# The end of a transformer block on one Trainium2 core: the norm's rows in groups of four blocks, each group in a PSUM bank of its own, and a square root of the first attention moved ahead of the last mask

## The chip, the core and the metric

The program runs on one core of one Trainium2 chip. Time is device microseconds (us) of one execution, from the first to the last instruction and what lies around them. The engines are TensorE (PE in the profile; PEld is its weight load), VectorE (DVE), ScalarE (ACT), GpSimd (POOL) and the DMA queue of SyncE (SP, SPq). Each runs its own list of instructions in order and waits on semaphores for the others.

## The reference, cut to what matters

Two transformer blocks follow one another, on 256 tokens of 1024 features in fp32. The change lies at the end of the first block's attention. The attention has two groups of heads, a retention and a difference of two softmaxes. Both are normed per head, joined, multiplied with `w_out`, gated and added to x; x is then normed and modulated, and a layer of product keys and experts begins with `hb @ w_query`.

```
x  = x + mod[:, 2] * (jnp.concatenate([ret_lat, diff_lat], axis=-1) @ w_out[layer])
h2 = modulate(x, norm2_g[layer], mod[:, 3], mod[:, 4])
x  = x + mod[:, 5] * peer_ffn(h2, peer_w_query[layer], ...)

def modulate(x, g, shift, scale):
    return rms_norm(x, g) * (1.0 + scale) + shift

out = merge_heads(rms_norm(y, g_norm) * (1.0 - lam_init))      # second group: diff_lat
scores = jnp.einsum('bhnid,bhnjd->bhnij', qc, kc) * intra_decay  # first group: a mask per head
```

## The kernel before, in words

Each fp32 product is made from two halves of each operand: ScalarE rounds a weight half of 128 x 1024 to `w_hi`, VectorE (for some halves GpSimd) subtracts to get `w_lo`, and TensorE runs three matmuls (hi by hi, hi by lo, lo by hi) into one PSUM region. The 257 weight chunks of 1 MB come in order through SyncE's queue into a ring of three (`raw`); chunk n waits until both halves of chunk n - 3 have been split. A half is numbered u: 40 to 47 are `w_out` (`U_OUT1`), 48 to 63 `w_query` (`U_QUERY`). On ScalarE and VectorE `ahead(u)` (L1401, L1853) makes every split up to half `REACH[u]`, about three beyond u; the ring of split halves has four places, so a split also waits for the matmuls of the half four before it.

The tokens are two tiles of 128 (i = 0, 1). The order of the attention is one list, `front_steps` (L149), which each engine walks for its own part of a step. `("win", p, h)` is a quarter of an input projection and brings `ahead` with it. `mask` n makes the decay mask of retention head n: VectorE two instructions, then ScalarE three exponentials; `madd` n is VectorE's sum of two of them. `rscore` n is TensorE's scores of head n, and VectorE's two products of scores and mask, which give the columns that `rweigh` n multiplies with v. `dvar`, `dnorm` are the norm of the second group: VectorE's scaling of sums, ScalarE's square root, VectorE's reciprocal and two products. `evac` 5 is ScalarE's silu of the last projection. `dblocks` transposes a gate and the four blocks of the second group (TensorE), which ScalarE and VectorE copy and split into `HC` (`high`, `low`); `out` n is the matmuls of half 40 + n of `w_out` with them. The last steps are `rweigh` 2 and 3, `rnorm`, `out` 2 and 3.

Then the four blocks of the first group are transposed (`block(TB_RET + k)`), each to a bank by `bank_of` (L788): banks 4, 5, 4, 5, so that the third waits until the first is split. `last_four` (L1049) runs the last four halves of `w_out`, first all for tile 0 (accumulators in banks 0, 1), then for tile 1 (banks 2, 3), with `turn_normed(0)` ahead of the last half of tile 1.

`normed` on ScalarE (L1461) and VectorE (L1928) is the end of the block. For a tile: VectorE adds the gated product to x (`add`, four instructions), ScalarE sums squares and takes the root (`squares`), VectorE inverts it and writes it on a diagonal (`inverse`), TensorE multiplies eight blocks of x by that diagonal (`turn_normed`, L1064), which transposes and scales them. Of each block an engine makes gain and shift (VectorE for even k, ScalarE for odd k) into `scaled4`, a ring of four, ScalarE rounds it into `HX`, and VectorE writes the rest. So a block passes three instructions and up to three waits. Tile 0 uses banks 0 and 1, tile 1 banks 2, 3, 0, 1 in turn (`norm_bank`, L774), with TensorE waiting for the blocks before. VectorE makes four blocks of tile 0, two of them ahead of `add(1)`, before it inverts the root of tile 1. The first half of `w_query` (`feat_half(48)`, L1130) needs, block by block, both tiles' rows in `HX`.

SyncE's queue has, between chunk 27 and chunk 28, the copy `x_keep <- x`, which waits for x of tile 1 (L820).

Of the kernel before, what the change touches and what calls it, by code (L numbers as in the profile page):

```python
# [7 lines left out]
F32 = mybir.dt.float32  # L8
# [140 lines left out]
def front_steps():  # L149
# [63 lines left out]
    win(5, 3, ("added", 1), ("rscore", 1), ("mask", 3), ("madd", 2), ("dnorm", 0), ("evac", 5))  # L213
# [156 lines left out]
def turned_at(i, k):  # L370

    return 8 * i + k + 1


def bank_turned(i, k):

    return turned_at(i, k if i else 7)


def both_turned(j, k):  # L380

    return 16 + 8 * (j - 1) + k + 1
# [5 lines left out]
def program(nc, wall, keys_d, cols_d, rows_d, bigrows_d, crow_d, wmod_d, dist_d, x_d, ctx_d, pT_d, gws_d, out_d, n_chunks):  # L388
    assert n_chunks * 2 == U_END
    with ExitStack() as es:  # L390
# [240 lines left out]
        scaled4 = fsc[:, 0:2, :].rearrange("p a (b t) -> p (a b) t", b=2)  # L631
# [142 lines left out]
        def norm_bank(i, k):  # L774

            if i == 0:
                return PB[k % 2][:, (k // 2) * 128:(k // 2 + 1) * 128]
            return PB[[2, 3, 0, 1][k % 4]][:, 0:128]
# [5 lines left out]
        def norm_half(s_, i, k):  # L784
            return HX[:, s_, k, i * 128:(i + 1) * 128]


        def bank_of(n):  # L788
            for first, banks in ((TB_Y, (4, 5, 6, 7)), (TB_U, (6, 7)), (TB_RET, (4, 5)),
                                 (TB_DIFF, (0, 1, 2, 3))):  # L790
                if n >= first:
                    return banks[(n - first) % len(banks)], n - len(banks) if n - first >= len(banks) else None
# [71 lines left out]
        def tensor_program(e):  # L864
# [199 lines left out]
            def turn_normed(i):  # L1064
# [3 lines left out]
                for k in range(8):  # L1068
                    if i and k >= 4:
                        t.wait_ge(s_nl, turned_at(1, k - 4))  # L1070
                    elif i and k >= 2:
                        t.wait_ge(s_nl, turned_at(0, 7))
                    t.did(mm(norm_bank(i, k), x[:, i, k * 128:(k + 1) * 128], dgn[:, i, :], True, True), s_nt)
# [56 lines left out]
            def feat_half(u, out, j=None):  # L1130
# [3 lines left out]
                for k in range(8):  # L1134
                    if j is not None:
                        t.wait_ge(s_nl, both_turned(j, k) if j else turned_at(1, k))
# [252 lines left out]
        def scalar_program(e):  # L1389
# [58 lines left out]
            def normed_highs(i, ks):  # L1448

                for k in ks:  # L1450
                    if k % 2:
                        a.wait_ge(s_nt, bank_turned(i, k))
                        if 8 * i + k >= 4:
                            a.wait_ge(s_nl, 8 * i + k - 3)
                        act(scaled4[:, k % 4, :], norm_bank(i, k), ACT.Identity, scale=G2[:, k:k + 1],
                            bias=modT[:, 24 + k, 0:1])
                    else:
                        a.wait_ge(s_nf, 4 * i + k // 2 + 1)
                    act(norm_half(0, i, k), scaled4[:, k % 4, :], ACT.Copy, sig=s_nh)

            def normed(last, scr_):  # L1461

                squares(N_PEER, 0, scr_)
                ahead(last - 2)
                ahead(last - 1)
                normed_highs(0, range(2))
                squares(N_PEER, 1, scr_)
                normed_highs(0, range(2, 8))
                ahead(last)
                normed_highs(1, range(8))  # L1470
# [349 lines left out]
        def vector_program(e):  # L1820
# [92 lines left out]
            def normed_lows(i, ks):  # L1913


                def difference(k):
                    v.wait_ge(s_nh, turned_at(i, k))
                    tt(norm_half(1, i, k), scaled4[:, k % 4, :], norm_half(0, i, k).bitcast(F32), SUB, sig=s_nl, free=True)

                for k in ks:  # L1920
                    if k % 2 == 0:
                        v.wait_ge(s_nt, bank_turned(i, k))
                        ts(scaled4[:, k % 4, :], norm_bank(i, k), G2[:, k:k + 1], modT[:, 24 + k, 0:1], MUL, ADD, sig=s_nf)
                    if k > ks[0]:
                        difference(k - 1)
# [791 lines left out]
```

## Time and profile before

| | us |
|---|---|
| median of three runs | 1788.83 |
| fastest and slowest of the three | 1788.52, 1795.13 |
| the profiled execution | 1793.46 |
| its span | 1791.7 |

| engine | busy us | share |
|---|---|---|
| TensorE | 1666.4 | 93% |
| VectorE | 1254.2 | 70% |
| ScalarE | 909.8 | 51% |
| GpSimd | 84.2 | 5% |

The profiled execution took 4.6 us more than the median, 1.8 of it outside its span. TensorE's busy time is that of an engine whose instructions overlap, so it is no measure of full speed; where it stands still, and at which clock it runs, says more. The mean granted clock is 0.97 of full speed.

### The profile page before, as it was taken

The page shows a single profiled execution, that of the slowest core. Times are in us where ns is not written, and L with a number is a line of the kernel's source. Part 1 is how long each engine was busy: PE and PEld are TensorE (multiplying, and loading weights), DVE is VectorE, ACT ScalarE, POOL GpSimd, SP SyncE. Part 2 cuts the span into 40 slices and gives each one's busy share as a digit, 9 for nine tenths or more (in the row PEclk, how much of TensorE's full clock was granted, in tenths as well). Part 3 has the DMA queues.
Part 4 walks back from the last instruction along what each step waited for, and adds up shares of the span by engine and source line. Part 5 has one row for each costly group of instructions (what it writes and reads, how often), then busy time and mean ns, then how long its engine had stood idle before and what let it go on. Part 6 is the DMA issues. An engine that isn't in the chain of part 4 may idle for free.

```text
span 1791.7 us, 29060 instructions
## 1 busy us (share of the span) xinstructions
PE 1666.4 (93%) x11518; PEld 1492.9 (83%) x11518; DVE 1254.2 (70%) x2040; ACT 909.8 (51%) x1206; POOL 84.2 (5%) x50
## 2 busy tenths in 40 slices
PE   6898787999999899988999999999998888999996
PEld 6676566998999788867999999899998777899995
DVE  5886655899888899976666555665556885655555
ACT  3454445554555455534444444544446766544445
POOL 1100002622000000000000000000000000000000
PEclk9898888999999999999999999999999998999998
DMA  6743333446655355637555555454543532555541
GB/s 262 275 168 133 106 110 123 144 165 200 205 182 199 141 201 202 220 133 267 211 199 211 198 189 186 154 200 177 191 185 130 212 130 106 190 193 188 188 171 64
DMA packets 53418, 318.52 MB, mean 178 GB/s; under 512 B 5953, under 2 KB 6113, under 8 KB 19362
## 3 DMA queue, kind: packets, MB, share of 16 engines
q1 hardware_dynamic: 52098, 310.60, 48.7%
q0 software_dynamic: 1184, 6.05, 0.9%
q8 instruction: 91, 1.49, 0.3%
q14 instruction: 45, 0.37, 0.1%
HBM read 307.17 MB, written 9.47 MB: 177 GB/s over the span
## 4 chain that ended last, share of the span: by engine, by line
PE 61%; DVE 25%; ACT 10%; issue 2%; DMA 2%; DVEq 0%; SPq 0%; ACTq 0%
PE pb L868 60%; DVE w_lo L1827 7%; DVE ar L1827 7%; ACT w_hi L1399 4%; ACT ar L1399 3%; DVE ar L1839 2%; DMA raw<-in_wall 1%; DVE HC L1827 1%; DVE ar L2181 1%; ACT L1399 1%; ACT HC L1399 1%; DVE ar L2178 1%; DVE ar L1984 1%; DVE raw L1984 1%; DVE ar L1981 1%
## 5 line engine op out<-in xcount | busy, mean ns | idle before, releaser
L1827 DVE TENSOR_TENSOR w_lo<-raw,w_hi 128x1024 fp32r<-128x1024 f32 x467 | 572.3, 1225 | 277.3 <-ACT w_hi L1399 251.8
L868 PE MATMUL pb<-HX,w_hi 128*128 128x256 f32 x3904 | 716.7, 285 | 12.2 <-DVE w_lo L1827 10.7
L1399 ACT ACTIVATE w_hi<-raw 128x1024 fp32r<-128x1024 f32 x498 | 528.2, 1061 | 346.2 <-PE pb L868 297.9
L868 PEld LDWEIGHTS pb<-HX,w_hi 128*128 128x128 f32 x3904 | 614.0, 193 | 19.7 <-DVE w_lo L1827 10.3
L868 PE MATMUL pb<-HX,w_lo 128*128 128x256 f32 x1952 | 553.9, 284 | 0.0
L868 PE MATMUL pb<-w_hi,HC 128*128 128x512 f32 (+1 forms) x1648 | 530.8, 393 | 11.7 <-DVE HC L1827 11.2
L868 PEld LDWEIGHTS pb<-HX,w_lo 128*128 128x128 f32 x1952 | 375.9, 193 | 0.0
L868 PEld LDWEIGHTS pb<-w_hi,HC 128*128 128x128 f32 x1648 | 312.0, 190 | 76.4 <-DVE w_lo L1827 12.5
L868 PE MATMUL pb<-w_lo,HC 128*128 128x512 f32 (+1 forms) x824 | 322.4, 391 | 0.0
L1827 DVE TENSOR_TENSOR ar<-ar 128x512 bf16<-128x512 bf16 (+8 forms) x470 | 247.5, 563 | 59.3 <-ACT ar L1399 30.9
L1399 ACT ACTIVATE ar<-pb 128x512 f32<-128x512 f32 (+3 forms) x203 | 112.7, 555 | 242.6 <-PE pb L868 154.9
L868 PE MATMUL pb<-w_hi,HX 128*128 128x512 f32 x512 | 177.7, 416 | 13.2 <-DVE w_lo L1827 5.6
L868 PEld LDWEIGHTS pb<-w_lo,HC 128*128 128x128 f32 x824 | 156.6, 190 | 29.4
L868 PE MATMUL pb<-ar 128*128 128x64 bf16 (+3 forms) x1960 | 134.1, 228 | 26.4 <-DVE ar L1827 8.7
L868 PEld LDWEIGHTS pb<-ar 128*128 128x128 bf16 (+2 forms) x1960 | 111.7, 124 | 50.7 <-issue 26.8
L868 PEld LDWEIGHTS pb<-w_hi,HX 128*128 128x128 f32 x512 | 102.4, 200 | 38.2 <-issue 11.4
L1399 ACT ACTIVATE HC<-ar 128x512 fp32r<-128x512 f32 x87 | 55.0, 632 | 103.8 <-PE pb L868 60.7
L868 PE MATMUL pb<-w_lo,HX 128*128 128x512 f32 x256 | 104.4, 408 | 0.0
L1827 DVE TENSOR_TENSOR HC<-ar,HC 128x512 fp32r<-128x512 f32 x87 | 60.3, 693 | 46.6 <-ACT HC L1399 42.8
L2565 POOL TENSOR_TENSOR w_lo<-raw,w_hi 128x1024 fp32r<-128x1024 f32 x31 | 75.7, 2442 | 158.5 <-ACT w_hi L1399 117.9
L1399 ACT ACTIVATE ar<-ar 128x512 f32<-128x512 f32 (+7 forms) x85 | 50.3, 591 | 57.5 <-DVE ar L1839 23.8
L868 PEld LDWEIGHTS pb<-w_lo,HX 128*128 128x128 f32 x256 | 51.3, 201 | 9.7
(139 smaller groups left out, 716.1 us busy)
## 6 DMA issues: line engine op xcount, KB each, us to landing
raw<-in_wall SPq DMA_DIRECT2D x257, 1024.0 KB, 4.8
ar<-in_wmod SPq DMA_DIRECT2D x24, 512.0 KB, 3.7
act_keep<-ar SPq DMA_DIRECT2D x28, 256.0 KB, 5.6
ar<-act_keep SPq DMA_DIRECT2D x28, 256.0 KB, 5.1
x<-in_wmod SPq DMA_DIRECT2D x8, 512.0 KB, 3.3
ar<-in_bigrows POOLq DMA_DIRECT2D x2, 1024.0 KB, 5.1
ar<-acs_keep POOLq DMA_DIRECT2D x2, 1024.0 KB, 8.4
ar<-in_crow SPq DMA_DIRECT2D x2, 512.0 KB, 5.9
```

The lines of the kernel that those rows point to most:

```text
L868: return e.matmul(o, l, r, start=start, stop=stop, skip_group_check=True)
L1399: a.did(e.activation(out, in_, func, scale=scale, **kw), sig)
L1827: v.did(e.tensor_tensor(out, a_, b_, op), sig)
L1839: v.did(e.scalar_tensor_tensor(out, a_, s_, b_, op0, op1), sig)
L1981: v.did(e.scalar_tensor_tensor(junk, w, 1.0, crow_ctx, MUL, MUL, accum_out=modT[:, n, 1:2]))
L1984: v.did(e.scalar_tensor_tensor(w, w, 1.0, c_, MUL, MUL, accum_out=modT[:, n, 0:1]), s_modv)
L2178: v.did(e.max(vals[:, c_], src))
L2181: v.did(e.max_index(idx[:, c_], vals[:, c_], src))
L2565: p.did(e.tensor_tensor(w_lo[:, made % NH, :], raw_half(w), w_hi[:, made % NH, :].bitcast(F32), SUB), s_lop)
```

## The change

Five edits. In the list of steps, `dnorm` and `evac` 5 go ahead of `mask` 3 and `madd` 2, `dnorm` also ahead of `rscore` 1. The four blocks of the first group get banks 4, 5, 7, 6. VectorE's splits of the half that `ahead(43)` makes (half 46) move behind the second of those blocks' splits. The norm's rows of a tile get two banks, even k in one and odd k in the other, for each tile its own; a wait is for four blocks, `scaled8` keeps all sixteen (in space that `qT` takes later), and the rounding and its rest are one instruction for four blocks. On VectorE `add(1)` comes ahead of all `low`s of tile 0, and the splits of halves 49 and 50 come last; on ScalarE the split of half 49 comes after `squares` of tile 1. The first `feat_half` takes k in the order 0, 2, 4, 6, 1, 3, 5, 7.

```diff
-    win(5, 3, ("added", 1), ("rscore", 1), ("mask", 3), ("madd", 2), ("dnorm", 0), ("evac", 5))
+    win(5, 3, ("added", 1), ("dnorm", 0), ("rscore", 1), ("evac", 5), ("mask", 3), ("madd", 2))
...
-        scaled4 = fsc[:, 0:2, :].rearrange("p a (b t) -> p (a b) t", b=2)
+        scaled8 = qTf[:, 0:2048].rearrange("p (i k t) -> p i k t", i=2, k=8)
...
         def norm_bank(i, k):
-            if i == 0:
-                return PB[k % 2][:, (k // 2) * 128:(k // 2 + 1) * 128]
-            return PB[[2, 3, 0, 1][k % 4]][:, 0:128]
+            return PB[2 * i + k % 2][:, (k // 2) * 128:(k // 2 + 1) * 128]
...
-            for first, banks in ((TB_Y, (4, 5, 6, 7)), (TB_U, (6, 7)), (TB_RET, (4, 5)),
+            for first, banks in ((TB_Y, (4, 5, 6, 7)), (TB_U, (6, 7)), (TB_RET, (4, 5, 7, 6)),
...
                 t.wait_ge(s_nd, 4 + i + 1)
-                for k in range(8):
-                    if i and k >= 4:
-                        t.wait_ge(s_nl, turned_at(1, k - 4))
-                    elif i and k >= 2:
-                        t.wait_ge(s_nl, turned_at(0, 7))
-                    t.did(mm(norm_bank(i, k), x[:, i, k * 128:(k + 1) * 128], dgn[:, i, :], True, True), s_nt)
+                for odd in range(2):
+                    for k in range(odd, 8, 2):
+                        ins = mm(norm_bank(i, k), x[:, i, k * 128:(k + 1) * 128], dgn[:, i, :], True, True)
+                    t.did(ins, s_nt)
...
-                for k in range(8):
+                for k in (0, 2, 4, 6, 1, 3, 5, 7) if j == N_PEER else range(8):
                     if j is not None:
-                        t.wait_ge(s_nl, both_turned(j, k) if j else turned_at(1, k))
+                        t.wait_ge(s_nl, both_turned(j, k) if j else group_turned(1, k % 2))
...
+            def normed_scaled(i):
+
+                a.wait_ge(s_nt, group_turned(i, 1))
+                for k in range(1, 8, 2):
+                    act(scaled8[:, i, k, :], norm_bank(i, k), ACT.Identity, scale=G2[:, k:k + 1], bias=modT[:, 24 + k, 0:1],
+                        free=k > 1)
+
+            def normed_highs(i):
+
+                a.wait_ge(s_nf, i + 1)
+                for odd in range(2):
+                    act(norm_group(0, i, odd), scaled8[:, i, odd::2, :], ACT.Copy, sig=s_nh)
 
             def normed(last, scr_):
 
                 squares(N_PEER, 0, scr_)
                 ahead(last - 2)
+                normed_scaled(0)
+                normed_highs(0)
+                squares(N_PEER, 1, scr_)
                 ahead(last - 1)
-                normed_highs(0, range(2))
-                squares(N_PEER, 1, scr_)
-                normed_highs(0, range(2, 8))
+                normed_scaled(1)
+                normed_highs(1)
                 ahead(last)
-                normed_highs(1, range(8))
...
+            def normed_scaled(i):
+
+                v.wait_ge(s_nt, group_turned(i, 0))
+                for k in range(0, 8, 2):
+                    ts(scaled8[:, i, k, :], norm_bank(i, k), G2[:, k:k + 1], modT[:, 24 + k, 0:1], MUL, ADD,
+                       sig=s_nf if k == 6 else None)
+
+            def normed_lows(i):
+
+                for odd in range(2):
+                    v.wait_ge(s_nh, group_turned(i, odd))
+                    tt(norm_group(1, i, odd), scaled8[:, i, odd::2, :], norm_group(0, i, odd).bitcast(F32), SUB, sig=s_nl,
+                       free=True)
...
                 ahead(last - 2)
-                ahead(last - 1)
-                normed_lows(0, range(2))
+                normed_scaled(0)
                 v.wait_ge(s_used, used(last))
                 add(1)
-                normed_lows(0, range(2, 4))
+                normed_lows(0)
                 inverse(N_PEER, 1)
-                normed_lows(0, range(4, 8))
-                normed_lows(1, range(8))
+                normed_scaled(1)
+                normed_lows(1)
+                ahead(last)
...
-                elif name == "out":
+                elif name == "out" and n < 3:
                     ahead(U_OUT1 + n)
...
-            turn(TB_RET, 4)
+            for k in range(4):
+                low(TB_RET + k)
+                if k == 1:
+                    ahead(U_OUT1 + 3)
             ahead(U_OUT1 + 4)
```

## Rows read from the trace of the kernel before

**Rows 1.** The chain that ended last, in order of time: start, us, what

```profile
240.55 12.54 PE pb L868 x64
...
291.02 54.14 PE pb L868 x442
```

**Rows 2.** TensorE in order of time: start, us, operation, count, [idle before, its releaser]

```profile
221.83 6.94 PE L868 MATMUL pb<-ar 64*128 64x256 f32 x24 [1.64 <-DVE ar L1839]
229.75 3.97 PE L868 MATMUL pb<-ar 64*128 64x256 f32 x24 [0.98 <-DVE ar L1839]
238.05 0.38 PE L946 MATMUL pb<-cols,modT 128*8 128x128 f32 x1 [4.33 <-ACT ar L1399]
```

**Rows 3.** TensorE, the same view: `rscore` 3, `out` 1, `rweigh` 2

```profile
244.58 1.99 PE L868 MATMUL pb<-ar 64*128 64x256 f32 x8
246.50 0.51 PE L868 MATMUL pb<-w_hi,HC 128*128 128x512 f32 x1
...
249.34 3.73 PE L868 MATMUL pb<-ar 128*128 128x128 f32 x32
```

**Rows 4.** ScalarE in order of time, around the last mask and the square root

```profile
225.96 1.06 ACT L1399 ACTIVATE w_hi<-raw 128x1024 fp32r<-128x1024 f32 x1
231.91 0.63 ACT L1399 ACTIVATE ar<-ar 128x512 f32<-128x512 f32 x1 [4.89 <-DVE ar L1839]
...
233.84 1.28 ACT L1399 ACT_TABLE_LOAD   x1
...
236.71 1.29 ACT L1399 ACTIVATE ar<-pb 128x512 f32<-128x512 f32 x2
```

**Rows 5.** VectorE in order of time, the same stretch

```profile
229.00 1.49 DVE L1839 SCALAR_TENSOR_TENSOR ar<-pb,ar 128x512 f32<-128x512 f32 x2
...
235.61 1.42 DVE L1827 TENSOR_TENSOR ar<-ar,sm 128x512 f32<-128x512 f32 x2
```

**Rows 6.** Windows of 2 us; the third number from the right is the granted clock

```profile
222.00:224.00 2.00, 2.00 (x7) 1.58 (x8) 1.81 (x3) 0.01 (x1) 0.00 (x0) 0.61 0.90 274
...
242.00:244.00 2.00, 2.00 (x8) 1.61 (x7) 1.23 (x1) 0.16 (x1) 0.00 (x0) 0.77 0.63 219
...
260.00:262.00 2.00, 0.43 (x3) 0.28 (x4) 1.81 (x3) 0.00 (x0) 0.00 (x0) 1.00 0.56 147
...
280.00:282.00 2.00, 0.00 (x0) 0.00 (x0) 1.05 (x2) 1.48 (x5) 0.00 (x0) 0.61 0.31 131
...
294.00:296.00 2.00, 2.00 (x18) 2.00 (x18) 1.86 (x2) 0.60 (x2) 0.00 (x0) 0.97 0.03 8
```

**Rows 7.** VectorE in order of time, at the first group's blocks

```profile
259.80 1.23 DVE L1827 TENSOR_TENSOR w_lo<-raw,w_hi 128x1024 fp32r<-128x1024 f32 x1
260.94 0.87 DVE L1839 SCALAR_TENSOR_TENSOR HC<-pb,cols,HC 128x256 fp32r<-128x256 f32 x2
```

**Rows 8.** TensorE in order of time, from there to the first half of `w_query`

```profile
261.56 0.80 PE L881 MATMUL pb<-cols,ar 128*128 128x128 f32 x4 [2.56 <-DVE HC L1839]
...
272.50 2.02 PE L868 MATMUL pb<-fsc,x 128*128 128x128 f32 x16 [0.58 <-DVE fsc L1832]
...
284.02 1.19 PE L868 MATMUL pb<-fsc,x 128*128 128x128 f32 x4 [8.08 <-DVE fsc L1832]
...
291.47 0.77 PE L868 MATMUL pb<-HX,w_hi 128*128 128x256 f32 x2
```

**Rows 9.** VectorE and ScalarE in order of time, in the norm

```profile
277.78 0.69 DVE L1827 TENSOR_TENSOR ar<-pb,ar 128x512 f32<-128x512 f32 x1
...
276.55 0.46 ACT L1399 ACTIVATE fsc<-pb,modT,sm 128x128 f32<-128x128 f32 x1
...
281.43 0.29 ACT L1399 ACTIVATE sm<-sm 128x1 f32<-128x1 f32 x1
```

**Rows 10.** SyncE's queue, and a DMA group (KB each, us to landing)

```profile
280.67 0.33 SPq L822 DMA_DIRECT2D x_keep<-x  x1
...
ar<-in_ctx SPq DMA_DIRECT2D x1, 1024.0 KB, 14.2
```

More of the change, by code:

```diff
@@ L367, in result, with group_turned @@
     return 4 * j + 2 * i + half + 1
[L370 to L377, printed above, removed]
+def group_turned(i, odd):
+    return 2 * i + odd + 1
 def both_turned(j, k):
-    return 16 + 8 * (j - 1) + k + 1
+    return 4 + 8 * (j - 1) + k + 1
 CTX_AT = {0: -256, 1: 256 - 512, 4: 768 - 2048, 5: 1280 - 2560}
@@ L774, in norm_bank, with norm_group @@
         def norm_bank(i, k):
-            if i == 0:
-                return PB[k % 2][:, (k // 2) * 128:(k // 2 + 1) * 128]
-            return PB[[2, 3, 0, 1][k % 4]][:, 0:128]
+            return PB[2 * i + k % 2][:, (k // 2) * 128:(k // 2 + 1) * 128]
         def rows_bank(k):
             return PB[k // 4 * 2 + k % 2][:, k // 2 % 2 * 256:k // 2 % 2 * 256 + 256]
-        def norm_half(s_, i, k):
-            return HX[:, s_, k, i * 128:(i + 1) * 128]
+        def norm_group(s_, i, odd):
+            return HX[:, s_, odd::2, i * 128:(i + 1) * 128]
         def bank_of(n):
-            for first, banks in ((TB_Y, (4, 5, 6, 7)), (TB_U, (6, 7)), (TB_RET, (4, 5)),
+            for first, banks in ((TB_Y, (4, 5, 6, 7)), (TB_U, (6, 7)), (TB_RET, (4, 5, 7, 6)),
                                  (TB_DIFF, (0, 1, 2, 3))):
@@ L1446, in squares @@
                 act(root_[:, i:i + 1], rs[:, 2 * i + 1:2 * i + 2], ACT.Sqrt, bias=part[:, i:i + 1], sig=s_std)
[L1448 to L1459, printed above, removed]
+            def normed_scaled(i):
[7 more added lines that the diff above has]
+                    act(norm_group(0, i, odd), scaled8[:, i, odd::2, :], ACT.Copy, sig=s_nh)
             def normed(last, scr_):
@@ L1911, in inverse @@
                 ts(dgn[:, i, :], ident, root_[:, i:i + 1], sig=s_nd)
[L1913 to L1925, printed above, removed]
-                difference(ks[-1])
+            def normed_scaled(i):
[8 more added lines that the diff above has]
+                       free=True)
             def normed(last, add):
```

## The prediction

> **What bounds the kernel now.** I read the chain of waits in order of time first, then the time orders of TensorE, ScalarE and VectorE from 216 to 312 us, then the windows. The chain lies on TensorE through `out` 0 to `rweigh` 3, and again for 54 us from 291.02 [rows 1]; between these it runs over ScalarE and VectorE, and there TensorE stands still. That is where the change works. TensorE waits 4.33 us until 238.05 for the silu of `evac` 5 [rows 2, 4], 2.56 us until 261.56 for the bank of the first group's first block, and 8.08 us until 284.02 for the diagonal of tile 1 [rows 8]. After 291 nothing in the stretch takes up a shift: VectorE's and GpSimd's work there hangs on TensorE's scores, so what is won ahead of 291 I carry to the end whole.
>
> Of the clock the rows show this. The windows have a mean of 0.61 in 222 to 224, where it falls to 1.2 GHz after TensorE was idle for 1.64 us and began on score products; 0.77 in 242 to 244, where it comes back, over 4 us after TensorE took up work at 238.05; 1.00 in 260 to 262 in spite of 2.56 us of idleness; 0.61 in 280 to 282, in the long stop; 0.97 in 294 to 296 [rows 2, 6, 8]. The same 24 records of `rscore` and `rweigh` take 3.97 us at full clock and 6.94 nearly all at the low one [rows 2].
>
> **Part A, `dnorm` and `evac` 5 ahead of mask 3.** ScalarE is free at 225.96 + 1.06 = 227.02 and then waits 4.89 us for mask 3 [rows 4]. Now a table load of 1.28 and a square root go there (done about 228.6), then the load for silu and the silu of 1.29 (done about 231.2); the exponentials of mask 3 may need a third load. TensorE's `evac` wait is thus gone. Against it, VectorE makes `dnorm`'s reciprocal and products (1.42 and some 0.3 around them) before `rscore` 1's products, which move from 229.00 to 230.75, and all behind them by 1.75: mask 3 begins on ScalarE at 233.65 instead of 231.91 [rows 4, 5]. A third load would run from 231.3 to 232.6, before the mask is there: nothing, with 1.0 us of cover left. The exponentials end at 235.5, `madd` 3 at 236.7.
>
> TensorE's `rscore` 2 moves from 229.75 to 231.5, after a gap of 2.7 instead of 0.98 us, and ends with `rweigh` 1 at 235.5 if the clock holds, at up to 238.4 if it falls (3.97 or 6.94 from there [rows 2]). `dblocks` began at 238.05. So `out` 0, which began at 240.55 [rows 1], begins 2.95 us earlier if the clock holds (`madd` 3 and two splits then end last, at 237.7), 0.1 to 0.3 earlier if it falls, and 0.9 us later at worst, if the first half of `rscore` 2 is slow too. The fall at 222 came after a shorter gap, before the same kind of products, so I take the fall. But TensorE is then busy from 231.5 on without the long stop, and the clock is back for `out` 0: that took 240.55 to 244.58 = 4.03 us, while `out` 1 took 246.50 to 249.34 = 2.84 [rows 1, 3]: 1.2 us won. **A = 0.15 + 1.2 = 1.35 us, bounds -0.9 and +4.1.** What is late next is TensorE itself.
>
> The Trainium skill, ScalarE: Activation LUTs, "What ACT_TABLE_LOAD costs", speaks against this reordering: it puts each switch of tables at 2.66 us, a drain on top of the load. Here two loads, a root and the gaps fit between 233.84 and 236.71, 2.87 us [rows 4], so no such drain is seen. By the page the exponentials would end about 3 us later, and A would be near 0; the row decides.
>
> **Part B, banks 4, 5, 7, 6.** The third and fourth block are transposed right behind the first two, which costs TensorE 0.7 us inside its wait. The split of half 46 took 1.23 us ahead of the first block's two splits, which ran 260.94 to 261.81 [rows 7]. Now they begin at 259.8 and TensorE's first half of `last_four` needs the first alone, while before it stood behind the fourth block, which waited for the second: it began about 262.1, and now 259.8 + 0.44 + 0.1 = 260.35, 1.75 us earlier. The moved split ends near 262.0, its half is wanted at 263.1; the split of half 47 (ScalarE at 261.0, VectorE at 262.95) ends at 264.2, its half is wanted at 264.4. That cover is thin: 0.2 us. **B = 1.75, bounds 1.4 and 1.9.**
>
> **Part C, the norm.** All times here are those of the trace, before the shifts. The diagonal of tile 0 is there at 272.4, TensorE's eight blocks end at 274.4 [rows 8]. VectorE splits half 48 alone until 274.3 (one of two splits leaves the path, 1.24 us), makes four scalings (0.45 apart, which is ScalarE's 0.46 for the same block [rows 9]: 276.1), and starts `add(1)` at 276.15 instead of 277.78 [rows 9]; TensorE's last half of `w_out` for tile 1 ends before that, 1.4 us (half of `out` 1) behind 274.4. ScalarE in that time makes four gains (0.46 each, overlapping by 0.09: 1.6) and two roundings of 128 x 512 (0.63 each by the nearest row of that size [rows 4]), and is free at 277.5, before the first half of x at 277.6. The root of tile 1, ended at 281.72 [rows 9], ends at 280.1. Then VectorE writes the diagonal at once (its two group splits lie before, under the root), at 280.95 instead of 283.87, where two more blocks stood ahead of it. TensorE starts tile 1 at 281.1 instead of 284.02 [rows 8].
>
> From there: before, 7.45 us to the first `w_query` matmul at 291.47. Now eight blocks at the low clock (2.02 at full clock, so 3.75 and some latency, until 284.9; the row of 1.19 for two of them agrees [rows 8]), four gains on ScalarE 1.6, rounding of the even group 0.65, its split 0.75 [rows 5], and 0.15 of latency: 288.1. The grouping itself wins next to nothing (0.4 us), because TensorE must finish all eight before ScalarE begins; the win is the diagonal's. So 3.3 us. The clock: before, TensorE was half busy from 284 and full speed came at about 294.1, 2.7 us into `w_query` [rows 6, 8]; now there is a gap of 3.2 us right before, so I allow up to 4 us of low clock, which costs 0 to 0.7 us more. **C = 3.0, bounds 1.8 (the whole first half at the low clock) and 3.9 (full clock within 1.5 us).** What is late next is again ScalarE's and VectorE's pass over tile 1. Of the splits that moved, half 49's ends at 290.0, wanted at about 292.5; half 50's at 291.3, wanted after 295. Behind them in SyncE's queue hangs chunk 27, which now starts when half 49 is split, at 290, and not at about 275.6 (two splits of 1.23 behind the rounding of half 48), with `x_keep` (280.67 [rows 10]) and chunk 28 behind it. Its first half, 54, is rounded once half 50 is used up: 288.1 and three halves of 2.9 us (54.14 us hold sixteen of them and their key scores [rows 1]) and 1 for the clock, about 298. That is a cover of 8 us. I cost it at nothing.
>
> **Sum.** 1.35 + 1.75 + 3.0 = 6.1 us. Against the profiled execution, 1793.46, that is 1787.4; the median of the runs lies 4.6 us lower, and against it 1788.83 - 6.1 = **1782.7 us**, 0.34% less. A measurement of this kernel tells about 0.5% (8.9 us) from no change.
>
> **The rivals.**
> 1. *The front gives back what it won.* VectorE's 1.75 us ahead of `rscore` 1 and a clock that stays low through `rweigh` 1 and `dblocks`: A = -0.9, the rest as above. 3.9 us, 1784.9. For it: 1.64 us were enough for the fall at 222 [rows 2, 6]. Against: TensorE has 6 to 7 us of work on end before `out` 0.
> 2. *The clock holds* in the 2.7 us gap, as in the 2.56 at 260 [rows 6, 8]: A = 4.1, C towards 3.5, 9.4 us, 1779.4, past the bound. Against: the work after that earlier gap was of full height, here it is products of 64 rows.
> 3. *Slower: chunk 27 lands late.* It has 8 us. The longest landing of a transfer of 1 MB was 14.2 us, with a full queue [rows 10]. Each us past 8 stops ScalarE's rounding and TensorE behind it; from 14.1 us on the sum of 6.1 is gone, and 23 us make the kernel over 0.5% slower, 1797.8. Here only `x_keep` and chunk 28 share the queue, and they come behind it.
> 4. *No shift reaches the end*: the VectorE chain from 345 us on or the ring of chunks takes it up: 1788.8. Against it: VectorE is idle up to TensorE's scores in all of the stretch before, as the chain's 54 us on TensorE say [rows 1].
>
> **How the numbers follow.** Forecast 0.58; rival 1 0.20; rival 2 0.11; rival 3 0.03; rival 4 0.08. The extremes of the bounds are 2.3 and 9.9 us, that is 1786.5 and 1778.9; three runs of one kernel were 6.6 us apart, upwards of the fastest, so the range is 1777 to 1789. Faster by over 0.5% is rival 2 and the edge of the forecast, where B and C come at their upper bounds: 0.18. Slower by over 0.5% is rival 3 and the spread: 0.03. Within 0.5%: 0.79.
>
> **What would show it.** Right: VectorE's products of `rscore` 1 come 1.75 us later than before, no 4.33 us stop of TensorE ahead of `dblocks`, full clock in `out` 0; no stop of 2.56 us at the first group's blocks; 15.6 us from TensorE's blocks of tile 0 (272.50) to the first `w_query` matmul (291.47), instead of 19.0 [rows 8]. Wrong: ScalarE waiting for chunk 27, a stop of TensorE for half 47 or 49, or a stretch from 291 to 345 that is longer than 54 us.

## The result, and the profile after

| | before | after |
|---|---|---|
| median of 20 runs each, us | 1794.97 | 1788.52 |
| lowest and highest | 1788.19, 1798.89 | 1784.83, 1794.38 |
| the profiled execution | 1793.46 | 1791.86 |
| its span | 1791.7 | 1790.1 |
| its mean granted clock | 0.970 | 0.967 |

The ratio is 0.9972, with a 95% interval of 0.9961 to 0.9982: the change wins 5.0 us (3.2 to 7.0), more than nothing and less than 0.5%. The two medians lie 6.4 us apart, inside that interval. I had said 6.1 us, and 1782.7 as the time. The size of the gain lies in the interval; the time is 5.8 us too low, because the median of three that I subtracted from, 1788.83, was a low draw of a kernel whose median over 20 runs is 1794.97. From that level 1782.7 would be a gain of 12.3 us, over twice the 5.0 measured. Of the 20 runs of before only three are under 1790, and two of the three that I had are among them.

The two profiled executions differ by 1.6 us only, which is less than the change wins in the stretch it touches. So first where the win stands, by points that both traces have. "Split" is the start of VectorE's split of half 41 at 219 us, the last work that the change leaves alone.

| us | before | after | won | said |
|---|---|---|---|---|
| A: split to `rscore` 3 | 24.84 | 24.19 | 0.65 | 1.35 |
| B: to the first addition to x | 23.30 | 21.44 | 1.86 | 1.75 |
| C: to the first `w_query` matmul | 23.59 | 20.05 | 3.54 | 3.3 |
| C, to the end of two `w_query` halves | 30.78 | 27.56 | 3.22 | 3.0 |
| from there to a memset of the expert layer | 439.10 | 438.09 | 1.01 | 0 |
| split to that memset | 518.02 | 511.28 | 6.74 | 6.1 |
| the mixer, first to last table load (about 1340 to 1567 us) | 221.93 | 226.82 | -4.89 | 0 |

A, B and C, to the end of two halves, win 5.73 us. The last 1.01 us up to the memset lies in work that the change leaves alone: in before the granted clock is 0.77 in 445 to 450 us and 0.89 in 450 to 455, in after it is 1.00 in both; in the eleven other kernels below the same piece takes 437.2 to 438.0 us.

TensorE in order of time, after, in the columns of [rows 2]:

```profile
221.00 3.97 PE L863 MATMUL pb<-ar 64*128 64x256 f32 x24 [1.65 <-DVE ar L1833]
230.68 7.33 PE L863 MATMUL pb<-ar 64*128 64x256 f32 x24 [5.71 <-DVE ar L1833]
237.84 0.27 PE L941 MATMUL pb<-cols,modT 128*8 128x128 f32 x1
...
240.17 0.47 PE L863 MATMUL pb<-w_hi,HC 128*128 128x512 f32 x1 [1.19 <-DVE HC L1833]
...
256.99 1.03 PE L876 MATMUL pb<-cols,ar 128*128 128x128 f32 x8
...
277.71 3.75 PE L863 MATMUL pb<-fsc,x 128*128 128x128 f32 x16 [5.13 <-DVE fsc L1826]
284.60 0.48 PE L863 MATMUL pb<-HX,w_hi 128*128 128x256 f32 x2 [3.14 <-DVE HX L1821]
```

The stop of 4.33 us ahead of `dblocks` is gone [rows 2], but the one ahead of `rscore` 2 has grown to 5.71 us. The stop of 2.56 us at the first group's blocks is gone, with the four blocks (eight records) in one piece at 256.99; 0.79 us is left behind them. The stop ahead of tile 1's blocks went from 8.08 to 5.13 us, and a new one of 3.14 stands in front of `w_query` [rows 8].

ScalarE in order of time, after, where the square root now stands:

```profile
226.26 1.28 ACT L1392 ACT_TABLE_LOAD   x1
227.56 0.21 ACT L1392 ACTIVATE sm<-sm 128x8 f32<-128x8 f32 x1
227.84 1.28 ACT L1392 ACT_TABLE_LOAD   x1
229.13 1.29 ACT L1392 ACTIVATE ar<-pb 128x512 f32<-128x512 f32 x2
230.50 1.28 ACT L1392 ACT_TABLE_LOAD   x1
232.83 0.63 ACT L1392 ACTIVATE ar<-ar 128x512 f32<-128x512 f32 x1 [1.05 <-DVE ar L1833]
```

The third load ends 1.05 us before mask 3 is there.

Windows of the clock, after, in the columns of [rows 6]:

```profile
226.00:228.00 2.00, 0.00 (x0) 0.00 (x0) 1.68 (x4) 1.84 (x4) 0.00 (x0) 0.87 0.00 0
228.00:230.00 2.00, 0.00 (x0) 0.00 (x0) 1.73 (x5) 1.90 (x3) 0.00 (x0) 0.50 0.00 0
```

In the 5.71 us stop the granted clock falls to 1.2 GHz, and the 24 records after it take 7.33 us.

TensorE's piece of the chain at `w_query` and behind it is 54.01 us, where it was 54.14 [rows 1]. At the memset after is 7.56 us ahead of before (730.20 against 737.76), of which 0.82 lay ahead of the split; at the first table load of the mixer it is 6.64 us ahead (1339.29 against 1345.93). In the mixer of the second block, which the change leaves alone, this one execution loses 4.89 us again. The same 24 matmuls behind the same stop, before and then after:

```profile
1451.43 2.89 PE L868 MATMUL pb<-ar 128*128 128x64 f32 x24 [1.96 <-DVE ar L1827]
```

```profile
1445.96 5.36 PE L863 MATMUL pb<-ar 128*128 128x64 f32 x24 [1.96 <-DVE ar L1821]
```

The windows of 5 us there, before and then after:

```profile
1445.00:1450.00 5.00, 4.47 (x20) 3.38 (x18) 4.55 (x6) 4.75 (x6) 0.00 (x0) 1.00 0.64 210
1450.00:1455.00 5.00, 3.56 (x28) 3.43 (x29) 4.82 (x4) 3.80 (x4) 0.00 (x0) 1.00 0.00 0
```

```profile
1445.00:1450.00 5.00, 4.04 (x19) 4.04 (x20) 4.79 (x5) 3.33 (x4) 0.00 (x0) 0.60 0.01 2
1450.00:1455.00 5.00, 5.00 (x16) 4.20 (x16) 4.65 (x5) 0.00 (x0) 0.00 (x0) 0.50 0.68 223
```

Once the clock stayed at 2.4 GHz, once it fell. From the table load ahead of this stop to the next it is 13.45 us in before (1447.93 to 1461.38) and 18.28 in after (1442.46 to 1460.74), so 4.83 of the 4.89 us are lost here. It is one of several places at which the mixer's time scatters, as the experiments show.

### The profile page after: what moved, and what is told of

Same layout as the page of the kernel before. It is cut to its first block, busy times and chain, and to the rows that moved or that the text cites. A ratio compares the mean times of both kernels' runs of the same rounds, so it can differ in the third digit from the quotient of the medians.

```text
span 1790.1 us, 29024 instructions
## 1 busy us (share of the span) xinstructions
PE 1668.2 (93%) x11518; PEld 1495.9 (84%) x11518; DVE 1252.1 (70%) x2028; ACT 908.1 (51%) x1195; POOL 83.5 (5%) x50
## 3 DMA queue, kind: packets, MB, share of 16 engines
q0 software_dynamic: 1184, 6.05, 0.8%
## 4 chain that ended last, share of the span: by engine, by line
PE 65%; DVE 20%; ACT 10%; DMA 2%; issue 2%; SPq 0%; DVEq 0%; ACTq 0%
PE pb L863 64%; DVE w_lo L1821 5%; DVE ar L1821 5%; ACT w_hi L1392 4%; ACT ar L1392 3%; DVE ar L1833 2%; DMA ar<-act_keep 1%; DVE ar L2177 1%; ACT L1392 1%; DMA raw<-in_wall 1%; ACT HC L1392 1%; DVE HC L1821 1%; DVE ar L1977 1%; DVE ar L2174 1%; DVE raw L1977 1%
## 5 line engine op out<-in xcount | busy, mean ns | idle before, releaser
L863 PE MATMUL pb<-w_hi,HC 128*128 128x512 f32 (+1 forms) x1648 | 530.0, 393 | 14.6 <-DVE HC L1821 12.3
```

The costliest lines, as they stand in the source:

```text
L863: return e.matmul(o, l, r, start=start, stop=stop, skip_group_check=True)
```

## The experiments

The theory: the three parts are independent stretches whose wins add, 0.65, 1.9 and 3.5 us; part A is small because VectorE's 1.75 us of `dnorm` stand ahead of `rscore` 1 and TensorE then runs `rscore` 2 and `rweigh` 1 at the low clock; part C is won by the order on VectorE, not by the groups. Its rivals: the parts overlap or depend on one another; A's loss has another cause; C is won by the groups. Each experiment is read by the stretches of the table above in its own trace, which are sharper than the times, and then by its time.

**The front alone.** The kernel before, with one line of the change.

```diff
-    win(5, 3, ("added", 1), ("rscore", 1), ("mask", 3), ("madd", 2), ("dnorm", 0), ("evac", 5))
+    win(5, 3, ("added", 1), ("dnorm", 0), ("rscore", 1), ("evac", 5), ("mask", 3), ("madd", 2))
```

> The kernel before with the list of steps reordered alone (root and evac 5 ahead of mask 3, root ahead of rscore 1). Measured on the stretch from VectorE's split that precedes the first head's score products to the start of rscore 3 on TensorE: 24.84 us in the trace before, 24.19 after the whole change. Theory 1 (TensorE's stop ahead of dblocks goes, but VectorE's 1.75 us ahead of rscore 1's products hold TensorE back at the low clock): 23.4 to 24.5, and the later stretches as before the change (23.3 us from rscore 3 to the first addition to x, 23.6 from there to the first w_query matmul). Theory 2 (the reordering is free, the clock came by chance): 20.7 to 22. Theory 3 (it costs): 25.5 or more. Time: 0 to 2 us less than before.

Measured: 1794.64 us, ratio 1.0008 (0.9997 to 1.0019). A took 24.21 us, as in after. But B took 24.98 and not 23.30: against the trace of before A won 0.63 us and B lost 1.68. TensorE in order of time and the windows, of this kernel:

```profile
260.16 0.80 PE L881 MATMUL pb<-cols,ar 128*128 128x128 f32 x4 [2.55 <-DVE HC L1839]
```

```profile
260.00:262.00 2.00, 1.84 (x9) 1.47 (x10) 1.20 (x4) 1.21 (x3) 0.00 (x0) 0.92 0.93 377
262.00:264.00 2.00, 2.00 (x6) 1.52 (x6) 1.33 (x2) 0.80 (x1) 0.00 (x0) 0.50 0.26 107
```

The stop of 2.55 us is the one of before [rows 8], but here the clock fell behind it, to 0.50 in 262 to 264, and `last_four` began slowly. In the trace of before it had stayed at full, 1.00 in 260 to 262 [rows 6]. Moving the front alone shows no gain in time.

**The banks alone.** The kernel before, with the banks and the later split of half 46.

```diff
-            for first, banks in ((TB_Y, (4, 5, 6, 7)), (TB_U, (6, 7)), (TB_RET, (4, 5)),
+            for first, banks in ((TB_Y, (4, 5, 6, 7)), (TB_U, (6, 7)), (TB_RET, (4, 5, 7, 6)),
...
-                elif name == "out":
+                elif name == "out" and n < 3:
...
-            turn(TB_RET, 4)
+            for k in range(4):
+                low(TB_RET + k)
+                if k == 1:
+                    ahead(U_OUT1 + 3)
```

> The kernel before with the four banks of the first group's blocks and the moved split of half 46 alone. From the start of rscore 3 to VectorE's first addition to x: 23.30 us before, 21.44 with the whole change. If the stop was the bank's and the split's alone: 21.4 to 21.6 here, and nothing in the other stretches. If part of it came from the shift of the other edits (clock, queue): 22 to 23.3. Time: 1.8 us less.

Measured: 1791.57 us, ratio 0.9991 (0.9981 to 1.0000). B took 21.44 us as in after, A and C (24.61, 23.60) about what they took before (24.84, 23.59). But its front, which has the old order, does not look like [rows 2]:

```profile
229.59 7.49 PE L868 MATMUL pb<-ar 64*128 64x256 f32 x24 [3.95 <-DVE ar L1839]
237.89 0.38 PE L946 MATMUL pb<-cols,modT 128*8 128x128 f32 x1 [0.81 <-ACT ar L1399]
```

Here `rscore` 1 and `rweigh` 0 took 3.97 us and not 6.94, so the stop ahead of `rscore` 2 is 3.95 us and not 0.98; the clock fell in it, `rscore` 2 and `rweigh` 1 took 7.49, and only 0.81 us of the 4.33 us stop ahead of `dblocks` is left. The next kernel has the same rows. In all twelve traces other than that of before the 24 records of `rscore` 1 and `rweigh` 0 took 3.97 us.

**The norm alone.** The kernel after, with the first two parts undone.

```diff
-    win(5, 3, ("added", 1), ("dnorm", 0), ("rscore", 1), ("evac", 5), ("mask", 3), ("madd", 2))
+    win(5, 3, ("added", 1), ("rscore", 1), ("mask", 3), ("madd", 2), ("dnorm", 0), ("evac", 5))
...
-            for first, banks in ((TB_Y, (4, 5, 6, 7)), (TB_U, (6, 7)), (TB_RET, (4, 5, 7, 6)),
+            for first, banks in ((TB_Y, (4, 5, 6, 7)), (TB_U, (6, 7)), (TB_RET, (4, 5)),
...
-            for k in range(4):
-                low(TB_RET + k)
-                if k == 1:
-                    ahead(U_OUT1 + 3)
+            turn(TB_RET, 4)
```

> The kernel before with the new norm alone (groups of four in banks of their own, second tile added first, moved splits). From the first addition to x to the first w_query matmul: 23.59 us before, 20.05 with the whole change. If the norm's edit stands by itself: 19.9 to 20.2 here. The first two halves of w_query may hold up to 1 us more of the low clock than before. Time: 2 to 3.5 us less.

Measured: 1791.66 us, ratio 0.9977 (0.9968 to 0.9987). C took 20.03 us, as in after; A 24.60; B 24.96, for here too the clock fell behind the old stop. A window of this kernel:

```profile
262.00:264.00 2.00, 2.00 (x7) 1.56 (x7) 1.25 (x3) 1.50 (x2) 0.00 (x0) 0.62 0.63 266
```

So the parts do not depend on one another: each shortens its own stretch alone as it does with the others, A by 0.63, B by 1.86 and C by 3.56 us, in sum 6.05, against 0.65, 1.86 and 3.54 with all of them. By time the three ratios sum to -0.24%, the whole is -0.28%, each known to about 0.1% only. The stretches next to the edited one do move, though by the clock: B rose by 1.7 us in two of the three. From the split to the memset the three kernels are shorter by 0.2, 3.3 and 2.9 us, in sum 6.4, and by 6.7 with all parts; that this fits so well is luck, because 1.0 to 1.9 us of each of these numbers is the piece behind `w_query`, which was slow in the trace of before. And B is worth more than its trace of before says: with the old banks it took 23.30 or 24.96 to 24.98, with the new ones 21.43 to 21.47 in the ten traces with them.

**Groups without the order.** The kernel after, with the split of half 49 and the differences of tile 0 ahead of `add(1)` again; on ScalarE, not shown, the split of half 49 goes ahead of tile 0's rows again.

```diff
                 ahead(last - 2)
+                ahead(last - 1)
                 normed_scaled(0)
+                normed_lows(0)
                 v.wait_ge(s_used, used(last))
                 add(1)
-                normed_lows(0)
```

> The changed kernel with the grouping kept and the order undone: both splits ahead of tile 0's scaling, tile 0's group splits ahead of the addition for tile 1. Theory 1 (the order wins, the grouping nothing): the addition for tile 1 starts 2.5 to 3.5 us later than in the changed kernel, and the stretch from the first addition to x to the first w_query matmul is 23.0 to 24.0 us, that of the kernel before. Theory 2 (the grouping wins by fewer waits): 21.5 or less. Time: 2.5 to 4 us more than the changed kernel.

Measured: 1792.01 us, ratio 0.9984 (0.9975 to 0.9994). C took 23.22 us: of the 3.54 us only 0.37 are left. From the diagonal of tile 1 to the first `w_query` matmul it is 7.32 us, as in after, against 7.89 before. In its parts, the 3.54 us of C are 1.55 from `add(0)` to `add(1)` (9.90 to 8.35), 1.42 from `add(1)` to the diagonal (5.80 to 4.38) and 0.57 behind the diagonal. In this kernel they are 11.72, 4.18 and 7.32 us. So the 0.57 us stay with the groups, and without the order the first two parts together win nothing. This is not the order of before: all of tile 0 is ahead of `add(1)` here and nothing of it behind, so `add(1)` comes 1.82 us later than there, and the diagonal follows sooner. TensorE in order of time, of this kernel:

```profile
279.47 3.75 PE L863 MATMUL pb<-fsc,x 128*128 128x128 f32 x16 [8.30 <-DVE fsc L1826]
286.36 0.77 PE L863 MATMUL pb<-HX,w_hi 128*128 128x256 f32 x2 [3.14 <-DVE HX L1821]
```

The long stop ahead of tile 1's blocks is back, 8.30 us, as before's 8.08 [rows 8].

**The root ahead of mask 3, but behind `rscore` 1.** The kernel after, with one step moved.

```diff
-    win(5, 3, ("added", 1), ("dnorm", 0), ("rscore", 1), ("evac", 5), ("mask", 3), ("madd", 2))
+    win(5, 3, ("added", 1), ("rscore", 1), ("dnorm", 0), ("evac", 5), ("mask", 3), ("madd", 2))
```

> The changed kernel with dnorm behind rscore 1 instead of ahead of it (order: added, rscore 1, dnorm, evac 5, mask 3, madd 2). If VectorE's 1.75 us ahead of rscore 1's products are what hold TensorE back: those products start 1.7 us earlier, rscore 2 and rweigh 1 with them, and the stretch from the split ahead of the first score products to the start of rscore 3 is 22.4 to 23.0 us instead of 24.19. If mask 3 and madd 3, which stay where they are, bind instead: 23.8 to 24.3. Time: 0 to 1.7 us less than the changed kernel.

Measured: 1787.58 us, ratio 0.9955 (0.9939 to 0.9971). A took 22.72 us, 1.47 less than after. TensorE in order of time, of this kernel:

```profile
221.48 3.97 PE L863 MATMUL pb<-ar 64*128 64x256 f32 x24 [1.62 <-DVE ar L1833]
229.40 7.49 PE L863 MATMUL pb<-ar 64*128 64x256 f32 x24 [3.95 <-DVE ar L1833]
...
239.23 0.47 PE L863 MATMUL pb<-w_hi,HC 128*128 128x512 f32 x1 [0.41 <-DVE HC L1833]
```

The stop is 3.95 instead of 5.71 us, 1.76 less, which is `dnorm`'s time on VectorE. The clock falls all the same and the 24 records still take 7.49 us. ScalarE's order and its three table loads are those of after. The two kernels with the old front have the same stop and the same 7.49 us, and A took 24.61 and 24.60 there: `dnorm` and `evac` 5 ahead of mask 3 win 1.9 us, and `dnorm` ahead of `rscore` 1 gives 1.5 to 1.7 of it back (A is 24.19 to 24.43 in the five traces that have it there without idle matmuls in front).

**Tile 1 block by block, the order kept.** The kernel after, with single waits for tile 1 and banks 2, 3, 6, 7 in turn; tile 0 keeps its groups. The diff is TensorE's part; ScalarE and VectorE do gain, rounding and rest of tile 1 for each block.

```diff
         def norm_bank(i, k):
+            if i:
+                return PB[[2, 3, 6, 7][k % 4]][:, 0:128]
             return PB[2 * i + k % 2][:, (k // 2) * 128:(k // 2 + 1) * 128]
...
+                if i:
+                    for k in range(8):
+                        if k >= 4:
+                            t.wait_ge(s_nl, block_turned(k - 4))
+                        t.did(mm(norm_bank(1, k), x[:, 1, k * 128:(k + 1) * 128], dgn[:, 1, :], True, True), s_nt)
+                    return
...
-                for k in (0, 2, 4, 6, 1, 3, 5, 7) if j == N_PEER else range(8):
+                for k in range(8):
```

> The changed kernel with tile 1's norm block by block again (four banks in turn, a wait for each block, gain, rounding and split block by block), tile 0 in groups, the order of the change kept. Theory 1 (grouping makes TensorE, ScalarE and VectorE take turns, so it costs on tile 1): the first w_query matmul comes about 4 us behind the diagonal of tile 1 instead of 7.0, and the first half of w_query ends 2.5 to 4 us earlier, since the last block is then waited for. Theory 2 (waits per block cost what turns cost): 6.5 to 7.5 us, no difference. Time by theory 1: 2 to 4 us less than the changed kernel.

Measured: 1784.62 us, ratio 0.9945 (0.9929 to 0.9961). The diagonal of tile 1 to `w_query` takes 5.00 us instead of 7.32, and C 17.72: theory 1, with 2.3 us won to the end of two halves (27.56 to 25.28). TensorE in order of time, of this kernel:

```profile
276.31 4.92 PE L873 MATMUL pb<-fsc,x 128*128 128x128 f32 x16 [5.12 <-DVE fsc L1852]
280.88 0.77 PE L873 MATMUL pb<-HX,w_hi 128*128 128x256 f32 x2
```

The blocks take longer on TensorE, 4.92 instead of 3.75 us, since they wait for banks; but the first matmul of `w_query` follows without a stop, because the first blocks have been rounded and split by then. The groups' 3.14 us stop is the price of having all eight blocks and their gains before the first rounding, on the path that ends last. Single waits alone are not what helps: the kernel before had them too and took 7.89 us, because VectorE still had four blocks of tile 0 behind the diagonal, and TensorE stood 2.02 us at 287.23 for a bank that tile 0 held. Four banks and the new order came together with the single waits here; which of them is worth how much was not taken apart.

**TensorE kept at work.** The kernel after, with idle matmuls of an identity into an unused bank: 4 and 10 of them ahead of `rscore` 1 and 2, 10 ahead of tile 1's blocks and 5 behind.

```diff
+            def warm(bank, n):
+                for _ in range(n):
+                    mm(PB[bank][:, 0:128], ident, ident, True, True)
...
+                    if n in (1, 2):
+                        t.wait_ge(s_wev, group_done(1))
+                        warm(2, 4 if n == 1 else 10)
...
+            warm(5, 10)
...
+            warm(5, 5)
```

> The changed kernel with additional 128 x 128 matmuls of the identity into an unused bank, whose result nobody reads: 4 ahead of rscore 1, 10 ahead of rscore 2, 10 ahead of tile 1's blocks, 5 behind them. Each costs about 0.24 us at full clock, all inside TensorE's stops. If the low clock after the stops is what the remaining time hangs on: granted clock 1.00 throughout, rscore 2 and rweigh 1 in about 4 us instead of 7.3, tile 1's eight blocks in 2.0 instead of 3.75, the first half of w_query in 2.9 instead of 4.4; together 4 to 6 us less than the changed kernel. If the clock falls nevertheless, the additional matmuls run at half speed and cost 1 to 4 us.

Measured: 1785.12 us, ratio 0.9951 (0.9937 to 0.9964). TensorE in order of time, of this kernel:

```profile
225.16 2.40 PE L863 MATMUL pb<-cols 128*128 128x128 f32 x20
231.04 6.60 PE L863 MATMUL pb<-ar 64*128 64x256 f32 x24 [3.47 <-DVE ar L1842]
...
277.52 2.02 PE L863 MATMUL pb<-fsc,x 128*128 128x128 f32 x16 [2.87 <-DVE fsc L1835]
```

Ten (20 records, 2.40 us) were too few in front: 3.47 us of stop are left, and the products still take 6.60, so A is 23.64, only 0.55 less than after. In the norm ten were enough: tile 1's blocks take 2.02 us and not 3.75, and C is 18.30 instead of 20.05. The 4 to 6 us expected did not come: it is 3.4 by the medians, and 2.4 from the split to the memset (511.28 to 508.86).

**Both better orders.** Block by block for tile 1 (its diff is the one above), and with it:

```diff
-    win(5, 3, ("added", 1), ("dnorm", 0), ("rscore", 1), ("evac", 5), ("mask", 3), ("madd", 2))
+    win(5, 3, ("added", 1), ("rscore", 1), ("dnorm", 0), ("evac", 5), ("mask", 3), ("madd", 2))
```

> The changed kernel with both earlier edits together: dnorm behind rscore 1, and tile 1's norm block by block. They lie in different stretches, so they should add: 22.7 us from the split ahead of the first score products to rscore 3, about 5 us from the diagonal of tile 1 to the first w_query matmul. Stretch from that split to GpSimd's memset in the expert layer: 506 to 507.5 us (511.3 in the changed kernel, 518.0 before). Time: 4 us less than the changed kernel, ratio to before 0.993 to 0.996.

Measured: 1784.02 us, ratio 0.9933 (0.9910 to 0.9955). A is 22.76, B 21.46, C 17.72, each as in the kernel that had it alone. The two add up by the stretches; by the times they come out within the scatter of the single ones.

**All three.** The last one, with idle matmuls.

```diff
+                    if n in (1, 2):
+                        t.wait_ge(s_wev, group_done(1))
+                        warm(2, 4 if n == 1 else 12)
...
+            warm(5, 16)
```

> The kernel of e8 with additional 128 x 128 matmuls of the identity into unused banks, which nobody reads: 4 ahead of rscore 1, 12 ahead of rscore 2, 16 ahead of tile 1's blocks. If the low clock is what is left: full clock through rscore 2 and rweigh 1 (4 us for the 24 records instead of 7.5), and through tile 1's blocks and the first half of w_query. Stretch from the split to the memset: 502 to 505 us, time 2 to 4 us less than e8. If the clock falls all the same, as it did in the front of the previous such kernel, 0 to 1.5 us.

Measured: 1781.52 us, ratio 0.9934 (0.9910 to 0.9958). TensorE in order of time, of this kernel:

```profile
224.72 2.84 PE L873 MATMUL pb<-cols 128*128 128x128 f32 x24
228.83 5.19 PE L873 MATMUL pb<-ar 64*128 64x256 f32 x24 [1.27 <-DVE ar L1868]
```

With the stop down to 1.27 us the 24 records take 5.19 instead of 7.49, not the 4 expected, and A falls to 20.90: 3.3 us less than after. C is 17.41, hardly less than 17.72, for block by block TensorE waits for the other engines anyway, and the clock is 0.50 again from 276 us on. Split to memset: 504.68 against 507.24.

**The mixer's stop.** The kernel after, with idle matmuls ahead of two groups of heads, which cover the stop at 1446.

```diff
+                    if n <= 4:
+                        t.wait_ge(s_xs, 8)
+                        warm(6, 3 if n == 0 else 7)
```

> The changed kernel with additional matmuls of the identity in the second block's mixer, far behind the change: 3 ahead of the first heads' products, 7 ahead of the next four's, in TensorE's stops of 0.6 and 2.0 us there. The stretch between the first and last table load of that part has the same work in every kernel so far and took 219.1 to 226.8 us (221.9 in the trace before, 226.8 in the changed one, where the clock fell at 1447 for 10 us). If the clock after that stop is what took the profiled gain back: 219 to 224 us here, no fall within 15 us of the heads' products, and 0 to 3 us less than the changed kernel in the mean. If something else took it: 224 to 228 us.

Measured: 1789.14 us, ratio 0.9973 (0.9958 to 0.9988), that of the change itself. The stop was closed and the clock held there, by TensorE in order of time:

```profile
1447.09 2.89 PE L863 MATMUL pb<-ar 128*128 128x64 f32 x24 [0.40 <-DVE ar L1828]
```

The mixer took 223.29 us all the same, with the clock falling at about 1355 to 1365 and 1485 to 1505, as near there in most traces. So the stop at 1446 explains the size of one loss in one execution, not the scatter of the mixer as a whole.

**All of it.** The kernel of all three, with the mixer's idle matmuls.

> The kernel with dnorm behind rscore 1, tile 1's norm block by block, additional matmuls of the identity in the front and the norm (4, 12 and 16), and those of the mixer (3 and 7). If the parts add: split to memset 503 to 506 us, the mixer's stretch 219 to 223 us, time 8 to 14 us less than the kernel before (ratio 0.992 to 0.9955), and not more than the kernel without the mixer's.

Measured: 1780.40 us, ratio 0.9919 (0.9902 to 0.9936), 14.5 us less than before and some 8 less than the change. A is 20.90, B 21.44, C 17.43: the stretches repeat to 0.03 us. That it is below the kernel of all three is no win of the mixer's idle matmuls: the intervals overlap, and alone these won nothing.

## Why the prediction was right or wrong

Two terms failed. The larger is the level, 1788.83 us, from which the sum was subtracted: it measured 1794.97, 6.1 us more, which is all of the miss in the time. The other is A, 1.35 us, which measured 0.65; its step that failed is the gap ahead of `rscore` 2, taken as 2.7 us and measured as 5.71. B, C and the bound came out as stated.

**The bound.** Right. TensorE's stops between 219 and 285 were the place; what was won up to `w_query` was still there at the memset at 730 us and, but for 0.9 us, at 1339 us. Rival 4 did not happen.

**A, size too large: 0.65 us, said 1.35.** Three of its steps held. VectorE's products of `rscore` 1 came 1.75 us later against the split (9.26 to 11.01); the third table load was hidden, with 1.05 us of cover (said 1.0); `out` 0 ran at full clock, from its start to `rscore` 3 2.94 us instead of 4.03, 1.09 won (said 1.2). The step that failed is the gap ahead of `rscore` 2. I took it as 2.7 us by adding 1.75 to the 0.98 of before [rows 2]. But in that trace `rscore` 1 and `rweigh` 0 ran at the low clock, 6.94 us [rows 2]; in after they ran at full, 3.97 us, and ended 3 us earlier, while their successor waits for VectorE. The gap was therefore 5.71 us, the clock fell in it, and `rscore` 2 with `rweigh` 1 took all of 7.33 us at 1.2 GHz. `out` 0 began 0.44 us later against the split (21.25 and 20.81), where I had said 0.15 earlier. I had taken the fall of the clock, so the gap's size explains at most 0.39 of the 0.70 us missing, 7.33 less 6.94; 0.11 is `out` 0, and the other 0.2 lies between `rweigh` 1 and `out` 0. That is rival 1 in mechanism, short of its price of -0.9; rival 2 did not happen, for the clock fell. The deeper fault is that [rows 2] were a rare draw, the only one of thirteen traces in which `rscore` 1 ran at the low clock: in the two kernels of the batch that leave A alone the old order has a stop of 3.95 us and `rscore` 2 at the low clock, and A is 24.60 and 24.61, against which the change wins 0.2 to 0.4 us. The stop of 4.33 us that it was to remove is 0.81 us there. The root behind `rscore` 1 shows what the position of `dnorm` costs, 1.5 to 1.7 of its 1.75 us; the idle matmuls show what the clock costs, 1.9 more (22.76 to 20.90).

**B, right: 1.86 us, said 1.75, with luck in the level.** The wait for half 47 cost nothing visible: the matmuls of `last_four` follow each other in 260 to 264 at a clock of 1.00. What I took as a property, that the 2.56 us of idleness leave the clock alone [rows 6, 8], was one draw: in the two other kernels with the old banks it fell behind them and B took 24.96 and 24.98. So the banks win 1.9 or 3.5 us, as the clock goes. It fell with the old front and with the new one, so the front's edit is not what made it fall.

**C, right: 3.54 us to `w_query` (said 3.3) and 3.22 to the end of two halves (said 3.0).** The mechanism was the stated one: `add(1)` starts 8.35 us behind `add(0)` instead of 9.90, 1.55 earlier (said 1.63); the diagonal follows the root at once, which is 1.42 more. From TensorE's blocks of tile 0 to the first `w_query` matmul it is 15.43 us (said 15.6). VectorE in order of time, after:

```profile
275.69 1.28 DVE L1821 TENSOR_TENSOR HX<-ar,HX 128x512 fp32r<-128x512 f32 x2
277.08 0.17 DVE L1845 RECIPROCAL sm<-sm 128x1 f32<-128x1 f32 x1
277.28 0.29 DVE L1826 TENSOR_SCALAR fsc<-cols,sm 128x128 f32<-128x128 f32 x1
```

The two group differences lie under the root. I put the grouping itself at 0.4 us; it is 0.57. What I did not see is that the step "TensorE must finish all eight" was a choice: with the win coming from the order, the groups could be dropped for tile 1, with four banks for it, and 2.3 us more be had. The low clock after the 3.14 us gap cost 0.3 us (3.54 less 3.22), inside the 0 to 0.7 I allowed.

**Chunk 27.** Rival 3 did not happen. SyncE's queue, after, and ScalarE's waits in 284 to 345 us (sum in us, count, longest):

```profile
258.35 28.50 SPq L836 DMA_DIRECT2D raw<-in_wall  x3
286.90 1.05 SPq L817 DMA_DIRECT2D x_keep<-x  x1
```

```profile
ACT ar L1392 <- PE pb L863: 16.2, 15, 1.8
ACT w_hi L1392 <- PE pb L863: 11.4, 9, 2.6
```

The first line groups three chunks; the last of them, chunk 27, ends the group at 286.85 us, right in front of `x_keep`, where I had said 290 before the shifts, 286.7 with the 3.3 us of them. And ScalarE waits for TensorE only, never for a transfer. The late start cost nothing. The rival was read too lightly, though: I took 14.2 us as the longest landing of 1 MB, but one weight chunk of the trace before took 16.0 us (4.8 in the middle), which is over the 14.1 us that I had worked out as the end of the gain.

**The sum and the level.** The sum of 6.1 us is 5.7 by the three stretches of these two traces and 5.0 (3.2 to 7.0) by the times. That A's missing 0.7 us shows so little in it is in part luck: B and C came 0.1 and 0.2 us over. Against the profiled execution, 1787.4 was said and 1791.86 measured: 5.7 us from the change, 1.0 ahead of the memset, 0.8 ahead of the split, less 0.9 up to the mixer, 4.9 in it and 0.1 behind, make the 1.6 us. Against the median it failed at the first term: three runs had a middle of 1788.83, twenty have 1794.97, and the profiled execution at 1793.46 was the better level. The predicted time would have been 1.1 us off had I subtracted from the profile alone.

**What stays open.** Why the clock falls behind a stop in one execution and not in the next. Eleven traces whose mixer does the same work (the changed one among them) have it at 219.1 to 226.8 us. The three shortest have a mean granted clock of 0.97 in it, the two longest of 0.92 and 0.93; nothing I changed decides which.

## What to carry to other kernels

When a step is moved in front of a waiting engine, work out the gap from when the engine in front will be ready in the new order, at both clocks, and not by adding the delay to the gap of one trace. Between engines that hand blocks to one another on the path that ends last, a wait for a group costs the time to fill it; groups belong where they are hidden. The distance between two points of a trace repeated to 0.1 us here where the clock did the same, while a median of three whole runs was off by 6. But one trace of the kernel before is one draw of the clock: its front, the stop of 2.56 us and the piece at 445 us all looked different in the next traces, by 1 to 3.5 us. Read a stop that a change is to remove in two traces before pricing it.

## What the runs showed of the hardware that was not expected

The granted clock answers to the same instructions differently from run to run. Behind the same stop of 1.96 us 24 matmuls took 2.89 or 5.36 us; behind 2.56 us the clock held in the trace of before and fell in two other kernels; behind 1.64 it fell [rows 2, 6] and behind 1.65 and 1.62, in after and with the root later, it held. The untouched mixer scatters by 7.7 us, from 219.1 us at a mean clock of 0.97 to 226.8 at 0.93, and in the 20 runs of after the executions with a span of 1783 to 1786 us have a mean clock of 0.968 to 0.972, those of 1789 to 1793 us 0.965 to 0.968. Idle matmuls in a stop bought part of the clock back: two places took the stretch from the split to the memset from 507.24 to 504.68 us.

A table load took ScalarE only its 1.28 us here and ran ahead of the wait of the instruction that needs it: the load at 230.50 lies in the wait for mask 3 and cost nothing. The Trainium skill, ScalarE: Activation LUTs, "What ACT_TABLE_LOAD costs", puts a switch at 2.66 us with a drain; two switches would be 5.3 us, as an estimate from the page. The trace of after does not agree: two loads, a root and the silu's start lie between 226.26 and 229.13, 2.87 us.
